# Hybrid attention and delta-rule layer on one core: where the modulation sums are kept, who splits the weights, and the order of every queue

## The chip, the cores and the metric

One of the eight cores of a Trainium2 chip runs the kernel. The metric is device time in microseconds (us) of one execution. Before the change it is 202.49 us, the median of three runs (202.23, 202.49, 203.05).

## The reference, cut to what matters

One layer over x of 256 rows and 1024 columns, batch 1, all in fp32:

```python
mod = silu(c) @ ada_w + ada_b                  # 1024 x 3072
shift, scale, gate = split(mod, 3)
h = rmsnorm(x, pre_norm_w) * (1 + scale) + shift
proj = h @ w_in                                # 1024 x 4104
# attention branch (8 heads of 64): rope on q and k, causal softmax, times silu(mg)
# delta branch (4 heads of 128, chunks of 64): short convolution over 4 rows, silu, l2 norm of
#   q and k, decays from db and da, solve of a 64 x 64 triangular system per chunk and head,
#   scan over the 4 chunks, rmsnorm, times silu(dz)
y = concat([o_moba, o_dn]) @ w_out             # 1024 x 1024
return x + gate * rmsnorm(y, post_norm_w)
```

## The kernel before, in words

Five engines run lists of calls that are written out by hand, one list each: SP issues the loads, PE (TensorE) multiplies, DVE (VectorE), ACT (ScalarE) and POOL (GpSimd) do the rest. An engine works strictly in the order of its list. A call waits for semaphores at its head, and all that stands behind it on its engine waits too.

**Split products.** fp32 products are made of three products of fp32r parts: each matrix is split in a high part (a copy, rounded to fp32r) and a low part (matrix minus high part), and `three` issues high*high, low*high and high*low. The weights come in 44 units. Unit n is copied to `whi` by ACT (`hi(n)`, L537) and its low part is made as `raw - whi` (`lo(n)`) by POOL (L459), or by DVE (L895) for the units that `DVE_LO` names: 41 to 43. Four split buffers are in turn, so `hi(n)` waits until PE has used unit n-4. Units 0 to 15 are the delta branch's q, k and v weights (384 KB, 768 columns, two units for each 128 rows of `w_in`), 16 to 35 are the rest of `w_in` (512 KB, 1024 columns), 36 to 43 are `w_out`.

**Modulation.** `silu(c) @ ada_w` for shift and scale is made in five pieces, which `PIECES` lists: pieces 0 and 1 give one 128-row block k of h each, pieces 2, 3 and 4 two. A piece has eight chunks (128 rows of `ada_w` each, 256 or 512 columns), loaded two at a time by `load_ada(p, g0, g1)`. DVE sums chunk times c_k over the chunks of `mod_sums` (L914, L916, L918); the running sum is in a PSUM bank (6 or 7), the last addition writes `acc` in SBUF. `mod(p)` on PE (L1341) then sums over partitions with a column of ones. Of piece 0 only chunks 0 and 1 go this way; chunks 2 to 7 are multiplied by PE itself with c as a one-column operand (`mod_direct`, L1333). `DVE_K` has the number of chunks that DVE sums. `modulate(p)` (DVE, L928 and L930) makes the scale and shift columns, `modulated(p)` (ACT, L580) applies them to the turned x, `h_hi(p)` (ACT, L585) and `h_lo(p)` (DVE, L885) split the result. `ada0` and `ada1` hold two pieces, so the loads of pieces 3 and 4 wait for the sums of pieces 1 and 2.

**Start.** x is scaled, turned by PE (`x_turn(b)`, L1325) into four banks and copied to `xT` by ACT (`xT_copy`) and DVE (`xT_move`). `qkv_products(n)` multiplies unit n (18 products of 256 columns) into six banks that hold all of q, k and v. Four of these banks held the turned x, so the first products wait for these copies. Unit n needs `h_lo` of its block and `lo(n)`. `busy(b, n)` issues products of ones that no one reads.

**Middle.** After `last_qkv_products`, `half(j)` multiplies unit 16+j (24 products of 256 columns); two halves make one of ten groups (attention q, k, v and the gates). Between the halves stand the small products of the delta branch: decays (`rows`, `cum`), the triangular inverse in levels 0 to 5 (`z_products`, `t_turn`, `x_products` on PE, `mask_z` and `merge` on DVE, `ti_copy` on ACT) for two row tiles, then the scan over four chunks; and the attention (`scores`, `probs`, `maxima`, `normalise`, `p_turn`, `pv`). `rope(r)` on DVE shuffles a group, POOL multiplies it by the sine (`rope_sin(r)`, L473), and DVE adds (L1061).

**End.** `y_products(k, t)` multiply `w_out` (6 products of 512 columns), `last_y_products` finish the second row tile, and `y_norm` and `finish` write the output.

## Time and profile before

| | before |
|---|---|
| median of three runs | 202.49 us |
| the profiled execution's own time | 202.14 us |
| its span, first to last instruction | 200.2 us |
| PE / DVE / ACT / POOL busy in the span | 188.3 / 135.5 / 103.7 / 95.1 us |
| DMA, mean over the span | 192 GB/s |
| mean granted TensorE clock | 0.982 of 2.4 GHz |

The profiled execution takes 1.94 us more than its span. Busy shares are averages over stages with different limits; a busy PE counts the modelled end of each product, and the products overlap: their starts in the trace stand 0.12 us apart where each shows 0.28 us. The granted clock has two levels, 1.0 (2.4 GHz) and 0.5 (1.2 GHz).

### The profile page before, as it was taken

The page shows a single profiled execution, that of the slowest core. Times are in us where ns is not written, and L with a number is a line of the kernel's source. Part 1 is how long each engine was busy: PE and PEld are TensorE (multiplying, and loading weights), DVE is VectorE, ACT ScalarE, POOL GpSimd, SP SyncE. Part 2 cuts the span into 40 slices and gives each one's busy share as a digit, 9 for nine tenths or more (in the row PEclk, how much of TensorE's full clock was granted, in tenths as well). Part 3 has the DMA queues.
Part 4 walks back from the last instruction along what each step waited for, and adds up shares of the span by engine and source line. Part 5 has one row for each costly group of instructions (what it writes and reads, how often), then busy time and mean ns, then how long its engine had stood idle before and what let it go on. Part 6 is the DMA issues. An engine that isn't in the chain of part 4 may idle for free.

```text
span 200.2 us, 4697 instructions
## 1 busy us (share of the span) xinstructions
PE 188.3 (94%) x1896; PEld 173.3 (87%) x1896; DVE 135.5 (68%) x315; ACT 103.7 (52%) x195; POOL 95.1 (47%) x51
## 2 busy tenths in 40 slices
PE   7998779999999989999999999999999999999970
PEld 6897769999999979989989998999899888788850
DVE  0657989472089976989868577938899256555364
ACT  3746344636379689754843432264651384463330
POOL 2037609795979348909372069540180072580000
PEclk9979999999999999999999999999999999999996
DMA  6999999997069800294300007105498735200022
GB/s 213 383 399 411 402 407 407 401 400 286 5 224 415 334 5 0 70 399 160 114 3 0 3 3 259 58 5 213 131 398 309 201 122 209 106 0 3 0 106 105
DMA packets 11527, 38.39 MB, mean 192 GB/s; under 512 B 1393, under 2 KB 1521, under 8 KB 10994
## 3 DMA queue, kind: packets, MB, share of 16 engines
q1 hardware_dynamic: 11362, 37.57, 49.5%
q10 hardware_dynamic: 144, 0.52, 0.7%
q8 instruction: 15, 0.25, 0.5%
q14 instruction: 6, 0.05, 0.1%
HBM read 37.04 MB, written 1.05 MB: 190 GB/s over the span
## 4 chain that ended last, share of the span: by engine, by line
PE 80%; DVE 15%; ACT 2%; issue 1%; POOL 1%; DVEq 0%; POOLq 0%
PE bank L1305 16%; PE bank L1307 15%; PE bank L1306 15%; DVE cv L941 6%; PE bank L1316 4%; DVE bank L916 3%; PE bank L1524 3%; PE bank L1513 3%; PE bank L1501 2%; PE bank L1325 2%; PE bank L1619 2%; PE bank L1595 2%; PE bank L1626 2%; PE bank L1561 1%; PE bank L1341 1%
## 5 line engine op out<-in xcount | busy, mean ns | idle before, releaser
L459 POOL TENSOR_TENSOR wlo<-raw,whi 128x1024 fp32r<-128x1024 f32 (+1 forms) x30 | 69.1, 2320 | 61.1 <-ACT whi L537 61.1
L1305 PE MATMUL bank<-hhi,whi 128*128 128x256 f32 x224 | 65.0, 290 | 2.5 <-DVE hlo L885 1.4
L1306 PE MATMUL bank<-hhi,wlo 128*128 128x256 f32 x224 | 63.3, 283 | 0.0
L1307 PE MATMUL bank<-hlo,whi 128*128 128x256 f32 x224 | 63.3, 283 | 0.0
L1305 PEld LDWEIGHTS bank<-hhi,whi 128*128 128x128 f32 x224 | 43.0, 192 | 4.1 <-DVE hlo L885 1.8
L1306 PEld LDWEIGHTS bank<-hhi,wlo 128*128 128x128 f32 x224 | 43.0, 192 | 0.0
L1307 PEld LDWEIGHTS bank<-hlo,whi 128*128 128x128 f32 x224 | 42.9, 191 | 0.0
L537 ACT ACTIVATE whi<-raw 128x1024 fp32r<-128x1024 f32 (+1 forms) x33 | 33.1, 1026 | 14.3 <-PE bank L1307 12.8
L941 DVE SCALAR_TENSOR_TENSOR cv<-bank,convh,cv 128x255 f32<-128x255 f32 (+2 forms) x36 | 17.0, 480 | 8.6 <-ACT cv L599 7.6
L916 DVE SCALAR_TENSOR_TENSOR bank<-ada,sml,bank 128x512 f32<-128x512 f32 (+1 forms) x24 | 16.5, 687 | 0.7
L1115 DVE SCALAR_TENSOR_TENSOR accg<-ada,sml,accg 128x512 f32<-128x512 f32 x16 | 13.6, 852 | 0.5
L1305 PE MATMUL bank<-whi,ohi 128*128 128x512 f32 x32 | 13.0, 406 | 0.0
L1306 PE MATMUL bank<-whi,olo 128*128 128x512 f32 x32 | 12.5, 390 | 0.0
L1307 PE MATMUL bank<-wlo,ohi 128*128 128x512 f32 x32 | 12.5, 390 | 0.0
L473 POOL TENSOR_TENSOR rot<-rot,cst 128x512 f32<-128x512 f32 x4 | 4.4, 1092 | 14.9 <-DVE rot L1057 11.7
L667 ACT ACTIVATE pr<-bank,stat 128x128 f32<-128x128 f32 (+1 forms) x16 | 6.5, 418 | 7.4 <-DVE stat L1082 7.4
L1316 PE MATMUL bank<-ones 128*128 128x256 f32 x26 | 8.5, 484 | 1.1 <-DVE ones L854 1.1
L580 ACT ACTIVATE bank<-xs,mod_b,mod_a 128x256 f32<-128x256 f32 x7 | 3.7, 561 | 10.7 <-DVE mod_a L930 10.7
L1305 PE MATMUL bank<-whi,hhi 128*128 128x256 f32 x32 | 9.1, 285 | 0.0
L1306 PE MATMUL bank<-whi,hlo 128*128 128x256 f32 x32 | 9.1, 283 | 0.0
L1307 PE MATMUL bank<-wlo,hhi 128*128 128x256 f32 x32 | 9.0, 283 | 0.0
L459 POOL TENSOR_TENSOR wlo<-cv,whi 128x768 fp32r<-128x768 f32 x4 | 7.3, 1846 | 2.2 <-ACT whi L537 2.0
(200 smaller groups left out, 359.2 us busy)
## 6 DMA issues: line engine op xcount, KB each, us to landing
raw<-in_w_rest SPq DMA_DIRECT2D x20, 512.0 KB, 5.6
ada<-in_ada SPq DMA_DIRECT2D x12, 512.0 KB, 9.0
ada<-in_gate_w SPq DMA_DIRECT2D x4, 1024.0 KB, 6.2
raw<-in_w_out SPq DMA_DIRECT2D x8, 512.0 KB, 4.5
ada<-in_ada SPq DMA_DIRECT2D x8, 256.0 KB, 6.1
raw<-in_w_qkv SPq DMA_DIRECT2D x5, 384.0 KB, 7.4
qkvs<-in_w_qkv SPq DMA_DIRECT2D x4, 384.0 KB, 9.4
cv<-in_w_qkv SPq DMA_DIRECT2D x4, 384.0 KB, 12.6
```

Of the source, the lines that this page charges most:

```text
L459: pool.tensor_tensor(split_u(wlo, n), raw_u(n), split_u(whi, n).bitcast(F32), ALU.subtract).then_inc(lo_done, 1)
L537: act.activation(split_u(whi, n), raw_u(n), ACT.Copy).then_inc(hi_done, 1)
L667: act.activation(pr[:, e, o:o + w], bank[ATT[e]][:, o:o + w], ACT.Exp, scale=AD ** -0.5, bias=stat[:, 16 + i:17 + i], accum_out=stat[:, 32 ...
L916: link(dve.scalar_tensor_tensor(a, w, c_k, a, ALU.mult, ALU.add))
L941: ins = dve.scalar_tensor_tensor(cv[:, i, j:], b[:, 0:S - j], w, cv[:, i, j:], ALU.mult, ALU.add)
L1115: dve.scalar_tensor_tensor(a, adag[:, k, :], sml[:, 24 + k:25 + k], a, ALU.mult, ALU.add).then_inc(gate_acc, 1)
L1305: pe.matmul(out, a[0][ia], b[0][ib], start=start, stop=False, skip_group_check=skip)
L1306: pe.matmul(out, a[1][ia], b[0][ib], start=False, stop=False, skip_group_check=skip)
L1307: return pe.matmul(out, a[0][ia], b[1][ib], start=False, stop=stop, skip_group_check=skip)
L1316: pe.matmul(bank[b][:, 0:256], ones[:, :], ones[:, 0:1].to_broadcast([P, 256]), start=True, stop=True)
L1513: ins = pe.matmul(blocks(3 + 2 * t, 0, CHUNK)[r, h, :], tt[r, t * DH + h, :], ident_of(c), start=True, stop=True)
L1524: ins = pe.matmul(blocks(2 + 2 * t, 256, HALF)[r, h, :], ti[r, i, :], zt[r, i, :], start=True, stop=True)
```

## The change

Five kinds of edit, made together:

1. `mod_sums` keeps the running sum in `acc` (SBUF) from the first chunk on. It no longer needs banks 6 and 7, so it no longer waits for `h_lo` of an earlier piece, only until `mod` has read `acc` of two pieces before.
2. Of pieces 1 and 2, chunks 6 and 7 are multiplied by PE (`mod_direct(p, k)`), as six chunks of piece 0 are; the bank that they write must be free (`mod_bank_free`). The loads of pieces 3 and 4 wait for these products too.
3. x block 0's turn moves ahead of chunks 6 and 7 of piece 0; the last two `busy` calls go.
4. The low parts of units 1 to 11, 13, 21, 26 and 37 move from POOL to DVE, that of unit 42 from DVE to POOL.
5. The lists of SP, ACT, DVE, PE and POOL get new orders. Units 1, 2 and 3 are loaded behind all of piece 2. On ACT `softplus` stands ahead of most tanh calls; on DVE `rope(0)` ahead of the silus; on PE the halves stand elsewhere among the small products, and the first two `y_products` are a little earlier.

The diff, cut to its core ("..." marks what is left out, all of it moved calls in the lists):

```diff
-        DVE_K = (2, 8, 8, 8, 8)
+        DVE_K = (2, 6, 6, 8, 8)
+
+        def directs(p):
+            return sum(NK - n for n in DVE_K[:p + 1])
...
-        DVE_LO = (41, 42, 43)
+        DVE_LO = (1, 2, 3, 4, 5, 6, 7, 8, 9, 10, 11, 13, 21, 26, 37, 41, 43)
...
                 if p == 3 and g0 == 0:
                     sp.wait_ge(acc_done, 2)
-                    sp.wait_ge(direct_done, NK - DVE_K[0])
+                    sp.wait_ge(direct_done, directs(1))
                 if p == 4 and g0 == 0:
                     sp.wait_ge(acc_done, 3)
+                    sp.wait_ge(direct_done, directs(2))
...
             load_ada(0, 2, 4)
+            load_ada(1, 0, 2)
             load_unit(0)
-            load_ada(1, 0, 2)
-            load_unit(2)
-            load_unit(1)
             load_ada(1, 2, 4)
-            load_unit(3)
             load_ada(2, 0, 2)
             load_ada(2, 2, 4)
+            load_unit(1)
+            load_unit(2)
+            load_unit(3)
+            load_ada(3, 0, 2)
             load_unit(4)
-            load_ada(3, 0, 2)
-            load_unit(6)
+            load_gates()
             load_unit(5)
             load_ada(3, 2, 4)
+            load_unit(8)
+            load_unit(6)
             load_unit(7)
-            load_unit(8)
             load_ada(4, 0, 2)
             load_unit(10)
+            load_gate_bias()
+            load_unit(12)
             load_unit(9)
             load_ada(4, 2, 4)
+            load_unit(16)
             load_unit(11)
-            load_unit(12)
...
             lo(31)
+            rope_sin(3)
             lo(32)
             lo(33)
             lo(34)
             lo(35)
             lo(36)
-            lo(37)
             lo(38)
             lo(39)
             lo(40)
+            lo(42)
...
             modulated(0)
-            xT_copy(0)
             h_hi(0)
+            xT_copy(1)
             xT_copy(2)
             hi(1)
+            xT_copy(0)
             hi(2)
             hi(3)
             modulated(1)
             h_hi(1)
-            xT_copy(1)
...
             conv_tanh(0)
+            softplus()
             conv_tanh(1)
             conv_tanh(2)
             conv_tanh(3)
-            softplus()
+            taps(4)
+            taps(5)
             hi(21)
...
-                n = 256 * PIECES[p][1]
-                a = bank[6 + p % 2][:, 0:n]
-                if p == 1 and k0 == 0:
-                    dve.wait_ge(mod_read, 1)
+                a = acc[:, p % 2, 0:256 * PIECES[p][1]]
                 if p >= 2 and k0 == 0:
-                    dve.wait_ge(hlo_done, p - 1)
-                for k in range(k0, k1):
+                    dve.wait_ge(mod_ready, p - 1)
+                for k in range(k0, min(k1, DVE_K[p])):
                     w, c_k = ada_piece(p)[:, k, :], sml[:, 24 + k:25 + k]
                     if k % 2 == 0:
                         dve.wait_ge(*ada_ready(p, k))
                     if k == 0:
-                        link(dve.tensor_scalar(a, w, c_k, None, ALU.mult))
-                    elif k < DVE_K[p] - 1:
-                        link(dve.scalar_tensor_tensor(a, w, c_k, a, ALU.mult, ALU.add))
+                        ins = dve.tensor_scalar(a, w, c_k, None, ALU.mult)
                     else:
-                        dve.scalar_tensor_tensor(acc[:, p % 2, 0:n], w, c_k, a, ALU.mult, ALU.add).then_inc(acc_done, 1)
+                        ins = dve.scalar_tensor_tensor(a, w, c_k, a, ALU.mult, ALU.add)
+                    if k < DVE_K[p] - 1:
+                        link(ins)
+                    else:
+                        ins.then_inc(acc_done, 1)
...
                 dve.wait_ge(mod_ready, p + 1)
+                dve.wait_ge(direct_done, directs(p))
                 if p == 0:
-                    dve.wait_ge(direct_done, NK - DVE_K[0])
                     dve.wait_ge(scale_done, 1)
...
             mod_sums(0, 0, 2)
             x_rstd()
             x_scale()
+            mod_sums(1, 0, 4)
             columns_in()
             modulate(0)
-            mod_sums(1, 0, 4)
             h_lo(0)
             xT_move(3)
-            mod_sums(1, 4, 8)
+            mod_sums(2, 0, 4)
+            mod_sums(1, 4, 6)
+            mod_sums(2, 4, 6)
+            lo(1)
             modulate(1)
-            mod_sums(2, 0, 4)
+            lo(2)
+            lo(3)
             h_lo(1)
-            mod_sums(2, 4, 8)
             mod_sums(3, 0, 2)
             modulate(2)
             mod_sums(3, 2, 4)
+            lo(4)
             h_lo(2)
+            lo(5)
             mod_sums(3, 4, 8)
+            lo(6)
             mod_sums(4, 0, 2)
             modulate(3)
+            lo(7)
+            lo(8)
             h_lo(3)
             mod_sums(4, 2, 4)
+            lo(9)
             mod_sums(4, 4, 8)
+            lo(10)
             ba_lo()
+            lo(11)
             modulate(4)
             h_lo(4)
+            lo(13)
...
-            conv_silu(0)
-            conv_silu(1)
             gates_in()
             rope(0)
+            conv_silu(0)
+            gates_out()
+            conv_silu(1)
             conv_silu(2)
-            gates_out()
             conv_silu(3)
             cum_copy()
             rope(1)
+            lo(21)
             conv(4)
...
             conv(5)
+            columns()
             conv_silu(4)
...
-            k_tokens(0)
             row_sum(0)
             maxima(0)
+            k_tokens(0)
+            k_tokens(1)
...
             decayed(0)
             decayed(1)
+            v_tokens(0)
+            v_tokens(1)
+            mask_z(0, 0)
+            mask_z(0, 1)
             gated_heads(0)
-            mask_z(0, 0)
+            mask_z(1, 0)
+            q_decayed(0)
+            mask_z(1, 1)
+            lo(26)
+            q_decayed(1)
...
             state_update(1)
             gate(2)
             gate(3)
+            o_sums(0)
+            lo(37)
             state_update(2)
-            gated_heads(3)
...
             lo(41)
-            lo(42)
             lo(43)
...
-            def mod_direct(k):
-
-                pe.wait_ge(sc_done, 1)
-                pe.wait_ge(*ada_ready(0, k))
-                for i in range(2):
-                    ins = pe.matmul(bank[7][:, i:i + 1], ada_piece(0)[:, k, i * P:(i + 1) * P], sml[:, 24 + k:25 + k],
-                                    start=(k == DVE_K[0] and i == 0), stop=False, skip_group_check=True)
+            def mod_bank_free(p):
+
+                if p == 1:
+                    pe.wait_ge(mod_read, 1)
+                if p >= 2:
+                    pe.wait_ge(hlo_done, p - 1)
+
+            def mod_direct(p, k):
+
+                if p == 0:
+                    pe.wait_ge(sc_done, 1)
+                if k == DVE_K[p]:
+                    mod_bank_free(p)
+                pe.wait_ge(*ada_ready(p, k))
+                for i in range(2 * PIECES[p][1]):
+                    ins = pe.matmul(bank[mod_bank(p)][:, i:i + 1], ada_piece(p)[:, k, i * P:(i + 1) * P], sml[:, 24 + k:25 + k],
+                                    start=(k == DVE_K[p] and i == 0), stop=False, skip_group_check=True)
                 ins.then_inc(direct_done, 1)
 
             def mod(p):
 
                 pe.wait_ge(acc_done, p + 1)
+                if DVE_K[p] == NK:
+                    mod_bank_free(p)
                 for i in range(2 * PIECES[p][1]):
                     ins = pe.matmul(bank[mod_bank(p)][:, i:i + 1], acc[:, p % 2, i * P:(i + 1) * P], ones[:, 0:1],
-                                    start=(p > 0), stop=True, skip_group_check=(p == 0))
+                                    start=(DVE_K[p] == NK), stop=True, skip_group_check=(DVE_K[p] < NK))
                 ins.then_inc(mod_ready, 1)
...
             busy(1, 3)
             busy(3, 8)
-            mod_direct(2)
-            mod_direct(3)
-            busy(2, 1)
-            mod_direct(4)
+            mod_direct(0, 2)
+            mod_direct(0, 3)
+            mod_direct(0, 4)
+            mod_direct(0, 5)
             mod(0)
-            mod_direct(5)
-            busy(0, 1)
-            mod_direct(6)
-            mod_direct(7)
             x_turn(0)
+            mod_direct(0, 6)
+            mod_direct(0, 7)
             x_turn(1)
             x_turn(2)
             x_turn(3)
             qkv_products(0)
+            mod_direct(1, 6)
+            mod_direct(1, 7)
+            mod_direct(2, 6)
             mod(1)
+            mod_direct(2, 7)
+            mod(2)
             qkv_products(1)
             qkv_products(2)
-            mod(2)
             qkv_products(3)
             qkv_products(4)
...
+            cum()
             k_turn(0)
-            cum()
-            k_turn(1)
             q_turn(0)
             q_turn(1)
+            k_turn(1)
             half(4)
```

## Rows read from the trace of the kernel before

**Rows 1.** The page, busy time of PE, and the engines' shares of the last-ending chain.
```profile
PE 188.3 (94%) x1896; PEld 173.3 (87%) x1896; DVE 135.5 (68%) x315; ACT 103.7 (52%) x195; POOL 95.1 (47%) x51
...
PE 80%; DVE 15%; ACT 2%; issue 1%; POOL 1%; DVEq 0%; POOLq 0%
```
**Rows 2.** Timeline of PE, 15 to 31 us: start, duration, work, [idle before, releaser].
```profile
18.35 0.61 PE L1341 MATMUL bank<-ones,acc 128*128 128x1 f32 x4 [0.58 <-DVE acc L918]
...
20.84 0.39 PE L1305 MATMUL bank<-hhi,whi 128*128 128x256 f32 x1 [1.07 <-ACT xs L567]
...
22.83 0.39 PE L1305 MATMUL bank<-hhi,whi 128*128 128x256 f32 x1 [0.29 <-DVE hlo L885]
...
25.86 1.05 PE L1341 MATMUL bank<-ones,acc 128*128 128x1 f32 x8 [0.61 <-DVE acc L918]
...
30.27 0.39 PE L1305 MATMUL bank<-hhi,whi 128*128 128x256 f32 x1 [1.11 <-DVE hlo L885]
```
**Rows 3.** The chain that ended last: the sums of piece 4 over partitions.
```profile
44.38 0.79 PE bank L1341 x8
```
**Rows 4.** Timeline of DVE, 13 to 43 us: sums of one-block and two-block pieces, h_lo.
```profile
16.25 1.53 DVE L916 SCALAR_TENSOR_TENSOR bank<-ada,sml,bank 128x256 f32<-128x256 f32 x3
...
29.53 0.69 DVE L885 TENSOR_TENSOR hlo<-bank,hhi 128x512 fp32r<-128x512 f32 x1 [0.37 <-ACT hhi L585]
30.13 2.33 DVE L916 SCALAR_TENSOR_TENSOR bank<-ada,sml,bank 128x512 f32<-128x512 f32 x3
...
42.47 0.75 DVE L918 SCALAR_TENSOR_TENSOR acc<-ada,sml,bank 128x512 f32<-128x512 f32 x1
```
**Rows 5.** Line L1115, the gate's sums in SBUF: count, shortest/median/longest ns.
```profile
L1115 DVE SCALAR_TENSOR_TENSOR accg<-ada,sml,accg x16: 740/752/2376, 128.7 to 154.7; 128x512 f32<-128x512 f32 x16
```
**Rows 6.** Timelines of ACT and PE, 10 to 22 us: unit 0, turned x, units 1 to 4.
```profile
10.21 0.84 ACT L537 ACTIVATE whi<-raw 128x768 fp32r<-128x768 f32 x1 [0.32 <-DMA raw<-in_w_qkv]
...
21.92 0.84 ACT L537 ACTIVATE whi<-raw 128x768 fp32r<-128x768 f32 x1 [1.13 <-DMA raw<-in_w_qkv]
...
12.01 3.60 PE L1325 MATMUL bank<-cst,xn 128*128 128x128 f32 x16
15.26 0.48 PE L1305 MATMUL bank<-hhi,whi 128*128 128x256 f32 x1
```
**Rows 7.** Stretches of 1 us: five engines busy, granted clock, DMA share, GB/s.
```profile
12.00:13.00 1.00, 1.00 (x7) 1.00 (x7) 0.72 (x3) 0.00 (x0) 0.94 (x1) 0.55 1.04 407
...
15.00:16.00 1.00, 1.00 (x8) 1.00 (x7) 0.44 (x2) 1.00 (x2) 0.00 (x0) 0.75 1.05 421
```
**Rows 8.** Timelines of POOL and DVE: the low parts of units, 768 and 1024 columns.
```profile
48.15 5.47 POOL L459 TENSOR_TENSOR wlo<-cv,whi 128x768 fp32r<-128x768 f32 x3 [2.02 <-ACT whi L537]
...
185.72 1.23 DVE L895 TENSOR_TENSOR wlo<-raw,whi 128x1024 fp32r<-128x1024 f32 x1 [2.85 <-ACT whi L537]
```
**Rows 9.** Timelines of POOL and DVE: calls of both engines that overlap in time.
```profile
42.31 1.85 POOL L459 TENSOR_TENSOR wlo<-rot,whi 128x768 fp32r<-128x768 f32 x1
...
117.95 7.49 POOL L459 TENSOR_TENSOR wlo<-raw,whi 128x1024 fp32r<-128x1024 f32 x3
...
43.52 0.73 DVE L890 TENSOR_TENSOR wbs<-wba,wbs 128x64 fp32r<-128x64 f32 x1 [0.29 <-ACT wbs L589]
...
118.09 2.80 DVE L1061 TENSOR_TENSOR kT<-rot 128x512 f32<-128x512 f32 x1 [0.76 <-POOL rot L473]
```
**Rows 10.** Timelines of DVE and PE, 55 to 76 us: the convolutions and what follows.
```profile
55.63 11.99 DVE L941 SCALAR_TENSOR_TENSOR cv<-bank,convh,cv 128x255 f32<-128x255 f32 x24 [7.56 <-ACT cv L599]
...
73.42 0.36 PE L1427 MATMUL bank<-zz,cst 128*128 128x8 f32 x2 [0.89 <-DVE zz L970]
...
75.64 0.36 PE L1305 MATMUL bank<-hhi,whi 128*128 128x256 f32 x1
```
**Rows 11.** The chain that ended last: half(8) from its start to the next call.
```profile
89.91 0.32 PE bank L1305
92.97 0.44 PE bank L1466 x4
```

More of the change, by code:

```diff
@@ L786, in _ @@
             decays(0)
+            factors()
+            v_copy(0)
+            hi(27)
             probs(0)
             decays(1)
[L789 removed]
             pT_copy(0)
[L791 removed]
+            ti_copy(1, 0)
+            ti_copy(1, 1)
+            probs(1)
             hi(28)
             hi(29)
[L794 to L796 removed]
             hi(30)
+            hi(31)
             ti_copy(2, 0)
             ti_copy(2, 1)
[L800 to L801 removed]
             ti_copy(3, 0)
             ti_copy(3, 1)
+            pT_copy(1)
             ti_copy(4, 0)
             hi(32)
[L806 removed]
             hi(33)
[L808 to L810 removed]
             ti_copy(4, 1)
             ti_copy(5, 0)
+            probs(2)
+            ti_copy(5, 1)
             v_copy(1)
+            heads_hi(0)
             pT_copy(2)
[L815 removed]
+            gate_tanh(1)
             wT_copy(0)
@@ L818, in _ @@
             hi(34)
+            wT_copy(1)
             hi(35)
+            heads_hi(1)
             probs(3)
-            wT_copy(1)
-            heads_hi(2)
+            hi(36)
+            hi(37)
+            vnew_copy(1)
             gate_tanh(2)
-            vnew_copy(1)
             pT_copy(3)
             gate_tanh(3)
-            hi(36)
-            hi(37)
+            hi(38)
             vnew_copy(2)
@@ L831, in _ @@
             vnew_copy(3)
-            hi(38)
+            hi(39)
+            heads_hi(2)
+            heads_hi(3)
             o_norm(1)
-            heads_hi(3)
-            hi(39)
             dn_hi(0)
+            hi(40)
             dn_hi(1)
-            hi(40)
             hi(41)
@@ L1249, in _ @@
             merge(2, 1)
-            rope(3)
             mask_z(3, 0)
             mask_z(3, 1)
-            gated_heads(1)
             merge(3, 0)
             merge(3, 1)
-            q_decayed(1)
+            rope(3)
+            gated_heads(1)
+            gate_sums(0, 0, 4)
             mask_z(4, 0)
             maxima(2)
-            gate_sums(0, 0, 4)
+            gate_sums(0, 4, 8)
+            merge(4, 0)
             mask_z(4, 1)
-            merge(4, 0)
-            normalise(2)
             mask_z(5, 0)
             merge(4, 1)
+            mask_z(5, 1)
+            normalise(2)
+            merge(5, 0)
+            gate_sums(1, 0, 4)
+            heads_lo(0)
             gate(1)
-            heads_lo(0)
-            merge(5, 0)
-            mask_z(5, 1)
-            gate_sums(0, 4, 8)
             gated_heads(2)
-            heads_lo(1)
             merge(5, 1)
@@ L1732, in _ @@
             half(8)
+            half(9)
             rows(1)
-            half(9)
+            kk_products(0)
+            kk_products(1)
             v_turn(0)
@@ L1737, in _ @@
             p_turn(0)
-            kk_products(0)
-            kk_products(1)
-            pv(0)
             z_products(0, 0)
             z_products(0, 1)
+            pv(0)
+            z_products(1, 0)
+            z_products(1, 1)
+            t_turn(1, 0)
+            t_turn(1, 1)
             scores(1)
+            x_products(1, 0)
+            x_products(1, 1)
             half(10)
             half(11)
-            z_products(1, 0)
-            t_turn(1, 0)
-            t_turn(1, 1)
-            z_products(1, 1)
-            x_products(1, 0)
-            x_products(1, 1)
+            p_turn(1)
+            z_products(2, 0)
             t_turn(2, 0)
-            z_products(2, 0)
             t_turn(2, 1)
@@ L1757, in _ @@
             x_products(2, 1)
+            z_products(3, 0)
             t_turn(3, 0)
             t_turn(3, 1)
-            z_products(3, 0)
             z_products(3, 1)
-            p_turn(1)
-            half(12)
-            pv(1)
             x_products(3, 0)
             x_products(3, 1)
+            t_turn(4, 0)
+            t_turn(4, 1)
             z_products(4, 0)
-            z_products(4, 1)
-            t_turn(4, 0)
+            pv(1)
+            half(12)
             scores(2)
@@ L1772, in _ @@
             half(13)
-            half(15)
             x_products(4, 0)
-            t_turn(4, 1)
+            z_products(4, 1)
             t_turn(5, 0)
@@ L1779, in _ @@
             x_products(5, 0)
+            z_products(5, 1)
             t_turn(5, 1)
-            z_products(5, 1)
+            half(15)
             p_turn(2)
```

129 lines of the change are left out of this document (44 added, 85 removed).

## The prediction

> **What bounds the kernel now.** I read the page first: PE is busy for 188.3 of 200.2 us, and the chain that ended last runs through PE for 80% of it [rows 1]. So only time in which PE stands still, or runs at the low clock, can be won; work moved between the other engines counts only by what PE waits for. The timeline of PE shows where it stands still: between its first unit product at 15.26 and 30.27 it waits five times, for sums (0.58 and 0.61), for a bank that still holds turned x (1.07) and for low parts of h (0.29 and 1.11), 3.66 us in all [rows 2]. From 30.27 on the timeline shows one more wait of note, 0.89 us at 73.42 for the decays [rows 10]. In between PE is never short of work: it comes to the sums of piece 4 at 44.38, though DVE had made them at 42.47 + 0.75 = 43.22 [rows 3, 4]. Last the stretches: the granted clock falls from 2.4 to 1.2 GHz at 12.1 us and is back at 15.5, in the middle of the stretch from 15 us [rows 7].
>
> The start is thus a race: PE's work until the sums of piece 4 ends at 44.38, and DVE is 1.16 us ahead of it. The change can give back PE's 3.66 us of waits only as far as DVE gets ready earlier, and it also gives DVE more to do.
>
> **The first product.** x is turned until 12.01 + 3.6 = 15.6 now, and unit 0 starts at 15.26 [rows 6]. With block 0's turn ahead of two chunks and two fillers gone, the 16 turns start near 10.3 and end near 13.8, the last eight at the low clock. Unit 0 is loaded behind two chunks of piece 1 (2 x 256 KB; at 400 GB/s, as the stretches show [rows 7], 1.3 us), so its high part starts at 10.21 + 1.3 = 11.5 and ends at 12.4; POOL's low part takes 1.82 us, a third of 5.47 [rows 8], and ends at 14.25. DVE's h_lo(0) ends near 14.05: it sums four chunks of piece 1 first (4 x 0.51 by 1.53 for three [rows 4], from 9.9 to 11.9), then modulates. Unit 0 starts at 14.3, 1 us earlier.
>
> **Loads.** Unit 4 lands at 21.9 [rows 6], behind units 1 to 3 and piece 2. The same bytes now come with the units last: unit 3 at 21.9 - 1.0 = 20.9, unit 2 at 19.9, unit 1 at 19.0. PE has no unit between 17.1 and 19. That costs nothing by itself, since DVE makes the sums of pieces 1 and 2 in this time, and PE's added work lies here as well: chunks 6 and 7 of pieces 1 and 2 are 8 + 16 one-column records, and four take 0.5 to 0.61 [rows 2], so 3.0 to 3.7 us, between 17.1 and 21.3.
>
> **DVE's queue from 14.05 to the last sum of piece 4.** I add it up, since I find no wait of more than a few tenths in it (each chunk lands before its turn):
> - xT_move: 0.6.
> - Sums: six of piece 2 and eight each of pieces 3 and 4, 22 x 0.78 = 17.2 (2.33 for three [rows 4]), and two of piece 1, 1.0. That these now read and write SBUF is priced at nothing: the gate's sums of the same width do so with a median of 752 ns [rows 5], against 750. The four sums taken off DVE (2 x 0.51 + 2 x 0.78 = 2.6) are already left out.
> - Low parts of units 1 to 9: no row shows 768 columns on DVE; 1024 take 1.23 [rows 8], 512 take 0.69 [rows 4], so 0.95, with starts 0.9 apart: 8.1. Bounds: the starts of 512 and of 1024 columns, 0.6 and 1.2, so 5.4 to 10.8.
> - modulate(1) to (3) 0.95, h_lo(1) to (3) 1.55.
>
> Sum 29.4, end at 43.45; now it is 43.22. DVE saves 2.6 and an earlier start, and spends 8.1 on low parts. PE meanwhile: h_lo(2) falls at 28.5 in this queue, unit 4 starts there and not at 30.27, units 4 to 9 take 6 x 2.16 (18 x 0.12) and the sums of piece 3 0.9, so PE is done at 42.4 and waits 1 us for DVE. mod(4) starts at 43.5 and not at 44.38: **lead 0.9 us**. Of the 3.66 us of waits three quarters come back as waits for DVE. With the bounds of the low part DVE ends between 40.8 and 46.2; below 42.4 PE sets the time, so the lead is between 2.0 and -1.8.
>
> **From there to 76 us.** Low parts on DVE take half as long as on POOL (0.95 for 1.82), PE needs one per 2.16 us: no wait. The convolutions, 11.99 us on DVE [rows 10], start with the last q, k, v products, so the lead goes through them. Behind them the order is new: gates_in 0.85, rope(0) 2.8, a silu 0.6, gates_out 0.35, three silus 1.8, the copy of the sums 0.2, then PE's three turns 1.4, as the same calls take now in other order. That is 8.0 us, no less than now (67.62 to 75.64), from the convolutions' end at 67.6 - 0.9 = 66.7, so the next half starts at 74.8 and not at 75.64 [rows 10]: lead 0.8. The wait of 0.89 becomes a wait for the silus.
>
> **Behind 76 us.** The amount of PE work is the same, only its order differs. A half that follows small products takes 92.97 - 89.91 = 3.06 [rows 11] against 24 x 0.12 = 2.88, 0.18 more; the change puts halves 8 and 9 side by side, which gives back one such entry, and lays three levels of the inverse bare that had a half between them. I take zero. The low part of unit 42 moves to POOL (2.4 for 1.23) some 2 us ahead of need; nothing waits. The tail is untouched.
>
> **Sum.** 202.14 - 0.8 = 201.3 for a profiled execution. This one lies 0.35 under the median, so the median goes from 202.49 to **201.7 us**; the likeliest case's own range is 200.6 to 202.4.
>
> **A rule weighed.** While POOL makes a low part, a DVE call with two SBUF inputs doesn't run: the 64-column L890 took 0.73 us, started at 43.52 and ended as POOL's call did (44.16), and L1061, 0.69 elsewhere, took 2.80 beside POOL's three [rows 9]. The Trainium skill says the same (SBUF — State Buffer, "SBUF: two separate sides"): the shared port pair is an exclusive lock, also for a DVE operation with two SBUF inputs against a GpSimd one that reads SBUF, and whichever starts first holds it for the whole instruction. By this rule the sums in SBUF are free only while POOL is idle, and it is from 14.3 to 44 us. The trace agrees. The places where POOL is not idle are the second rival.
>
> **Rivals.**
> - *The new orders give PE back its small gaps.* For: 0.18 us at each entry to a half, twelve halves behind 76 us, together 2.2. Against: it needs every handover to be covered better, and the levels laid bare are not. 201.7 - 2.2 = 199.5.
> - *DVE waits for POOL at the low part of unit 21 (slower).* DVE reaches lo(21) behind rope(1), at 76.2 by my walk; ACT ends the high part of unit 22 at 76.4, and POOL then holds SBUF for 2.4 us. If POOL comes first, lo(21) ends at 76.4 + 2.4 + 1.2 = 80.0 and not at 77.4; PE needs it at 74.8 + 2.9 = 77.7, and waits 2.3 us. It decides from a shift of 0.2 us. 201.7 + 2.3 = 204.0. The same can happen at ba_lo beside lo(12), near 44 us, for 0.5 to 1.3 us more. For: L1061 in [rows 9]. Against: order at this place is a near tie.
> - *The clock falls in the start.* Before 12.1 us PE did mostly one-column products, and the clock fell [rows 7]. PE now does such products, and waits, from 17.1 to 21.3. At 1.2 GHz from 18.9 to 25.7 units 1 and 2 take 4.3 each: PE reaches unit 4 near 30, lead 0.3, so 202.2. A single such stretch of 3.4 us is hidden by DVE's queue.
>
> **How the numbers follow.** A measurement here can tell about 0.5%, 1.0 us. Forecast 0.35, small gaps won 0.26, DVE behind POOL 0.27, clock 0.12. Faster by over 1.0: nearly all of the gaps case, and 0.4 of the forecast's, 0.14: 0.40. Slower by over 1.0: nearly all of the POOL case, and the low part's upper bound: 0.26. Within: 0.34. The range is 199.2 to 204.5.
>
> **What would show it.** After: unit 0 near 14.3; unit 4 near 28.5; PE waiting about 1 us for L1341 near 42.5 to 43.5 with DVE without idle time ahead of it; sums in `acc` at 0.75 us; low parts of 768 columns at 0.95. L895 for unit 21 at 1.2 us (3.6 would be the POOL case), and half(5) without idle time ahead. The granted clock between 18 and 26 us at 1.0, or 0.5 for the clock case. The forecast is wrong if DVE's queue isn't what mod(4) waits for, or if PE takes a different time from 76 us to its last product than the 118 us of now.

## The result: 214.5 us, 5.9% slower, and the profile after

The changed kernel takes 214.47 us (median of four runs, 213.50 to 215.30). The kernel before took 202.36 us beside it (202.14 to 203.05). The ratio is 1.059, with a 95% interval of 1.054 to 1.065. Here and below a median and a range are over all executions of a kernel, a ratio leaves out those more than 1.5% above its fastest. The forecast was 201.7 us, with a range of 199.2 to 204.5: wrong in sign and in size. The profiled execution took 213.66 us.

The page of the kernel after, its span, the busy times and the shares of the chain that ended last; to be read beside [rows 1]:

```profile
span 211.9 us, 4737 instructions
...
PE 194.4 (92%) x1916; PEld 178.9 (84%) x1916; DVE 149.9 (71%) x325; ACT 103.7 (49%) x195; POOL 69.6 (33%) x37
...
PEclk9999589999999999999999859999999999999996
...
PE 61%; DVE 18%; issue 7%; DMA 5%; ACT 4%; SPq 3%; POOL 1%; DVEq 0%; ACTq 0%
```

The span grew by 11.7 us, PE's busy time by 6.1 us. So about half of the loss is PE standing still, and the other half is PE being busy for longer. Part of that are the one-column products that it has taken over, the larger part is in the clock's row: the slices of 5.3 us each show 5 tenths at the fifth, and 8 and 5 at the 23rd and 24th. The chain has PE in it for 61% (80% before) and DVE for 18% (15%).

The waits of PE in the kernel after name the first half (engine and line, what it waited for, us in total, times, longest):

```profile
PE bank L1642 <- DVE pr L1080: 7.5, 1, 7.5
PE bank L1320 <- DVE ones L845: 1.1, 1, 1.1
PE bank L1455 <- DVE gcs L965: 0.9, 1, 0.9
```

One wait of 7.5 us: the turns of p (`p_turn(1)`, L1642) for `normalise(1)` on DVE (L1080), which scales the four p tiles of a head pair. Of line L1080 the trace of the kernel after gives the shortest, median and longest call:

```profile
L1080 DVE TENSOR_SCALAR pr<-pr,stat x16: 272/346/2448, 97.6 to 161.5; 128x128 f32<-128x128 f32 x8, 128x256 f32<-128x256 f32 x8
```

Sixteen calls, half of them under 0.35 us, and the longest, of 256 columns, 2.45 us where such a call takes 0.35 otherwise. The timelines of the kernel after at this place say why, DVE first, then POOL, ACT and PE (start, duration, work, [idle before, releaser]):

```profile
112.02 0.69 DVE L1051 TENSOR_TENSOR qT<-rot 128x512 f32<-128x512 f32 x1 [0.76 <-POOL rot L478]
112.63 0.17 DVE L1076 RECIPROCAL stat<-stat 128x4 f32<-128x4 f32 x1
112.84 9.35 DVE L1080 TENSOR_SCALAR pr<-pr,stat 128x128 f32<-128x128 f32 x4
122.11 0.47 DVE L1036 TENSOR_TENSOR tt<-tt,bank 128x128 f32<-128x128 f32 x2
...
110.83 1.09 POOL L478 TENSOR_TENSOR rot<-rot,cst 128x512 f32<-128x512 f32 x1 [12.65 <-issue]
112.68 9.35 POOL L464 TENSOR_TENSOR wlo<-raw,whi 128x1024 fp32r<-128x1024 f32 x4 [0.77 <-ACT whi L528]
...
111.54 2.96 ACT L528 ACTIVATE whi<-raw 128x1024 fp32r<-128x1024 f32 x3
114.85 1.06 ACT L528 ACTIVATE whi<-raw 128x1024 fp32r<-128x1024 f32 x1 [0.35 <-PE bank L1311]
...
114.48 0.28 PE L1311 MATMUL bank<-hlo,whi 128*128 128x256 f32 x1
...
122.24 1.11 PE L1642 MATMUL bank<-cst,pr 128*128 128x128 f32 x4 [7.48 <-DVE pr L1080]
```

Four scalings on DVE and four low parts on POOL take the same 9.35 us, from the same moment: each scaling waits until a low part is done (9.35 / 4 = 2.34 us), then the next low part starts, then the next scaling waits. The low parts take what they take alone (2.4 us), so DVE alone pays. Moves in two lists of the change open the door. On POOL `rope_sin(3)` stood ahead of `lo(29)` and waited for DVE's shuffle, and now stands behind `lo(31)`; `lo(28)` stood ahead of `rope_sin(2)` and now stands behind it, so that there are four low parts in a row. And `hi(28)`, `hi(29)` stood ahead of `probs(1)` on ACT and now stand behind it, so ACT delivers 28, 29 and 30 in one go from 111.54, just as DVE comes to `normalise(1)`. POOL and DVE of the kernel before, at the same place:

```profile
116.90 1.09 POOL L473 TENSOR_TENSOR rot<-rot,cst 128x512 f32<-128x512 f32 x1 [8.19 <-DVE rot L1057]
...
109.63 1.01 DVE L1090 TENSOR_SCALAR pr<-pr,stat 128x128 f32<-128x128 f32 x4
```

POOL stood idle for 8.19 us in front of `rope_sin(3)`, and in that idle time the four scalings ran in 1.01 us. What looks like a useless wait kept POOL out of DVE's way. Nor has PE other work in the kernel after: its list has `p_turn(1)` ahead of two levels of the inverse, whose `merge` (L1036) is queued behind the scalings on DVE as well.

The second half, in stretches of the kernel after (length, then per engine busy us (calls) in the order PE, PEld, DVE, ACT, POOL, then granted clock, DMA share, GB/s):

```profile
20.00:21.00 1.00, 1.00 (x10) 1.00 (x11) 1.00 (x3) 0.90 (x3) 0.00 (x0) 0.92 0.92 298
21.00:27.00 6.00, 6.00 (x29) 6.00 (x30) 5.86 (x14) 3.30 (x6) 0.00 (x0) 0.50 1.01 374
27.00:28.00 1.00, 1.00 (x7) 1.00 (x7) 0.55 (x2) 0.97 (x3) 0.00 (x0) 0.66 1.00 377
...
119.00:120.00 1.00, 0.00 (x0) 0.00 (x0) 1.00 (x2) 0.00 (x0) 1.00 (x2) 0.92 0.00 0
120.00:126.00 6.00, 3.76 (x48) 3.43 (x50) 2.87 (x4) 0.27 (x1) 2.03 (x1) 0.50 0.48 170
126.00:127.00 1.00, 1.00 (x31) 1.00 (x28) 0.00 (x0) 0.50 (x2) 0.00 (x0) 0.67 0.86 242
```

While PE stands still the clock goes to 1.2 GHz, at 119.8 (by the 0.92 of the stretch from 119), and stays there until 126.7. PE works from 122.2 to 126.7 at half rate: 4.5 us of time for 2.2 us of work, so 2.2 us more. The clock is low in the start as well, from 20.8 to 27.7, as the clock rival said; the low stretch that the kernel before has from 12.1 to 15.5 is not there in this execution.

The rest of the loss lies in the start. Timelines of DVE, POOL and PE of the kernel after, around the sums of piece 4, with PE's half(8) and its last product:

```profile
42.26 2.33 DVE L904 SCALAR_TENSOR_TENSOR acc<-ada,sml,acc 128x512 f32<-128x512 f32 x3
...
45.37 1.86 DVE L881 TENSOR_TENSOR wbs<-wba,wbs 128x64 fp32r<-128x64 f32 x1
47.15 0.95 DVE L886 TENSOR_TENSOR wlo<-rot,whi 128x768 fp32r<-128x768 f32 x1
...
57.38 1.00 DVE L931 SCALAR_TENSOR_TENSOR cv<-bank,convh,cv 128x255 f32<-128x255 f32 x2 [5.51 <-ACT cv L590]
...
44.92 2.23 POOL L464 TENSOR_TENSOR wlo<-cv,whi 128x768 fp32r<-128x768 f32 x1 [30.57 <-ACT whi L528]
...
44.74 0.95 PE L1357 MATMUL bank<-ones,acc 128*128 128x1 f32 x8
...
91.86 0.39 PE L1309 MATMUL bank<-hhi,whi 128*128 128x256 f32 x1
...
205.35 0.39 PE L1311 MATMUL bank<-wlo,ohi 128*128 128x512 f32 x1
```

mod(4) starts at 44.74 and not at 44.38 [rows 3]. `ba_lo` (L881, 64 columns) takes 1.86 us beside POOL's low part of unit 12 and pushes back the low part that PE needs next; the convolutions start at 57.38 and not at 55.63 [rows 10], half(8) at 91.86, where the timeline of before has 89.84: 2.0 us late. The stall adds 7.6 (114.48 to 122.24, less the 0.12 of a product), the clock behind it 2.2: 11.8 us in all. PE's last product moved from 193.72 to 205.35, by 11.6.

### The profile page after: what moved, and what is told of

Read it like the earlier page. It is cut to its first block, busy times and chain, and to the rows that moved or that the text cites. A ratio compares the mean times of both kernels' runs of the same rounds, so it can differ in the third digit from the quotient of the medians.

```text
span 211.9 us, 4737 instructions
## 1 busy us (share of the span) xinstructions
PE 194.4 (92%) x1916; PEld 178.9 (84%) x1916; DVE 149.9 (71%) x325; ACT 103.7 (49%) x195; POOL 69.6 (33%) x37
## 4 chain that ended last, share of the span: by engine, by line
PE 61%; DVE 18%; issue 7%; DMA 5%; ACT 4%; SPq 3%; POOL 1%; DVEq 0%; ACTq 0%
PE bank L1309 14%; PE bank L1311 13%; PE bank L1310 13%; DVE cv L931 5%; DMA ada<-in_ada 5%; DVE pr L1080 4%; SPq L342 3%; PE bank L1529 2%; PE bank L1540 2%; DVE wlo L886 2%; PE bank L1517 2%; DVE acc L904 2%; PE bank L1611 1%; PE bank L1642 1%; PE bank L1577 1%
## 5 line engine op out<-in xcount | busy, mean ns | idle before, releaser
L464 POOL TENSOR_TENSOR wlo<-raw,whi 128x1024 fp32r<-128x1024 f32 (+1 forms) x24 | 57.6, 2416 | 61.6 <-ACT whi L528 61.6
L1310 PE MATMUL bank<-hhi,wlo 128*128 128x256 f32 x224 | 64.6, 288 | 0.0
L1311 PEld LDWEIGHTS bank<-hlo,whi 128*128 128x128 f32 x224 | 44.2, 197 | 0.0
L904 DVE SCALAR_TENSOR_TENSOR acc<-ada,sml,acc 128x512 f32<-128x512 f32 (+1 forms) x25 | 17.1, 686 | 0.7
L464 POOL TENSOR_TENSOR wlo<-cv,whi 128x768 fp32r<-128x768 f32 x3 | 5.9, 1985 | 35.1 <-ACT whi L528 35.1
L886 DVE TENSOR_TENSOR wlo<-raw,whi 128x1024 fp32r<-128x1024 f32 (+1 forms) x9 | 9.8, 1100 | 5.5 <-ACT whi L528 5.5
L1080 DVE TENSOR_SCALAR pr<-pr,stat 128x128 f32<-128x128 f32 (+1 forms) x16 | 12.9, 864 | 0.1
L634 ACT ACTIVATE ti<-bank 128x256 f32<-128x256 f32 x10 | 3.8, 382 | 17.0 <-PE bank L1529 16.9
L1642 PE MATMUL bank<-cst,pr 128*128 128x128 f32 x24 | 4.1, 314 | 7.5 <-DVE pr L1080 7.5
L1642 PEld LDWEIGHTS bank<-cst,pr 128*128 128x128 f32 x24 | 3.1, 161 | 7.8 <-DVE pr L1080 7.7
```

The source lines that it names most:

```text
L464: pool.tensor_tensor(split_u(wlo, n), raw_u(n), split_u(whi, n).bitcast(F32), ALU.subtract).then_inc(lo_done, 1)
L886: dve.tensor_tensor(split_u(wlo, n), raw_u(n), split_u(whi, n).bitcast(F32), ALU.subtract).then_inc(dve_lo_done, 1)
L904: ins = dve.scalar_tensor_tensor(a, w, c_k, a, ALU.mult, ALU.add)
L1080: ins = dve.tensor_scalar(pr[:, e, o:o + w], pr[:, e, o:o + w], stat[:, i:i + 1], None, ALU.mult)
L1310: pe.matmul(out, a[1][ia], b[0][ib], start=False, stop=False, skip_group_check=skip)
L1311: return pe.matmul(out, a[0][ia], b[1][ib], start=False, stop=stop, skip_group_check=skip)
```

## Experiments

The theories have letters in the expectations. A: the 10 us behind 110 us come from POOL's pile of low parts meeting normalise(1), and the lower clock that follows from it. B: POOL has no part in it. C: the near tie of `ba_lo` with the low part of unit 12 (in experiment 5 C is another theory, told there, and in experiment 6 the tie is under A). D: TensorE's clock in the start. The times before in the same sets were 202.1 to 202.3 us.

**1. POOL yields to normalise(1).** The change, plus one wait on POOL:

```diff
             rope_sin(2)
+            pool.wait_ge(pn_done, 2)    # until normalise(1) is done
             lo(28)
```

> The changed kernel, with one wait more: POOL starts the low part of unit 28 only when normalise(1) on DVE is done. Theory A (port): in the changed kernel the four scalings of normalise(1) each wait for one of POOL's four low parts of units 28 to 31, 9.35 us where they take 1.0 otherwise, and PE's 7.6 us of idle time before p_turn(1) and the 1.2 GHz stretch behind it come from that. Then normalise(1) takes 1.0 us, PE's idle time goes, and the time is 214.5 - 7.6 - 2.2 = 204.7 us (203.5 to 206), 1 to 2% slower than before. Theory B (order): p_turn(1) and level 2 of the inverse stand too early in PE's list for DVE, whatever POOL does: the stall stays over 4 us and the time over 210.

Measured: 203.75 us (201.64 to 208.37, ten runs), ratio 1.003 (1.000 to 1.007). One wait gives back 10.7 of the 12.1 us. The timelines of this kernel, DVE and POOL:

```profile
111.03 1.01 DVE L1081 TENSOR_SCALAR pr<-pr,stat 128x128 f32<-128x128 f32 x4
```
```profile
112.12 9.32 POOL L464 TENSOR_TENSOR wlo<-raw,whi 128x1024 fp32r<-128x1024 f32 x4 [2.01 <-DVE pr L1081]
```

The four scalings take 1.01 us, the low parts their 9.32 as before, only behind them. A holds. From `p_turn(1)` to PE's last product this kernel takes 81.06 us (112.77 to 193.83) and the changed one 83.11 (122.24 to 205.35), 2.05 more, which is the price of the clock behind the stall, 2.2 by the sum above. In this execution `ba_lo` came first and took 0.22 us, the convolutions started at 55.61 and PE's last product at 193.83, against 193.72 before. Its clock was low in the start for 6.8 us in all, as in the changed kernel, but in two stretches, 11.2 to 14.7 and 21.5 to 24.9.

**2 and 3. Each half of the change alone.** The start of the change (up to the last q, k, v product) with the rest of before, and the reverse. The part that differs, beside the lists:

```diff
-        DVE_LO = (41, 42, 43)
+        DVE_LO = (1, ..., 11, 13, 41, 42, 43)   # front alone
+        DVE_LO = (21, 26, 37, 41, 43)           # back alone
```

> The change in the start alone: sums in SBUF, chunks 6 and 7 of pieces 1 and 2 on PE, the new orders up to the last q, k, v products, and the low parts of units 1 to 11 and 13 on DVE; from there on the lists of before. In the changed kernel the convolutions start 1.75 us later than before (57.38 against 55.63), so both theories expect 202.4 + 1.8 = 204.2 us (203.3 to 205). Were the start better than before once the rest is as it was, it would be under 202.

> The start of before, and from the last q, k, v products on the lists of the change (units 21, 26, 37 on DVE, 42 on POOL). Theory A: the meeting of normalise(1) with POOL's low parts is still there, so 202.4 + 7.6 + 2.2 = 212.2 us (210 to 213.5). If the meeting hangs on a shift of a microsecond at the start, it is under 207.

Measured: front alone 203.64 us (200.80 to 205.59, ten runs, four of them between 200.8 and 201.5 and none from there to 203.6), ratio 0.999 (0.995 to 1.003). Back alone 212.82 (212.03 to 214.84), ratio 1.053 (1.047 to 1.060). The waits of PE in the kernel with the back alone have the stall of the full change:

```profile
PE bank L1626 <- DVE pr L1088: 7.5, 1, 7.5
```

So the loss sits in the back half. The start has two values: four executions are about 1.1 us faster than the kernel before, six are 1.3 or more slower, and the median is that of the slower ones, just inside the 203.3 to 205 that I expected.

**4. The pile without the change.** The kernel before, with `rope_sin(3)` out of the way and `lo(28)` kept back, so that three low parts meet DVE in the same place:

```diff
-            lo(28)
             start_inverse()
             rope_sin(2)
-            rope_sin(3)
+            pool.wait_ge(rope_done, 3)
+            lo(28)
             lo(29)
             lo(30)
+            rope_sin(3)
             lo(31)
```

> The kernel before, in which POOL waits until rope(2) is done and then makes the low parts of units 28, 29 and 30 in a row (rope_sin(3) behind them): nothing else is changed, and PE needs unit 28 only some 15 us later. Theory A: three of the four scalings of normalise(1) each wait for 2.4 us, normalise(1) takes 7 to 8 us for 1.0, merge(1, 0) behind it on DVE is late, PE waits 5 to 7 us: 207 to 211 us. Theory B: POOL is a bystander, 202.4 us, within 0.5%.

Measured: 210.63 us (209.03 to 211.80), ratio 1.039 (1.034 to 1.043). The timelines of DVE and POOL, then the waits of PE:

```profile
109.34 7.31 DVE L1091 TENSOR_SCALAR pr<-pr,stat 128x128 f32<-128x128 f32 x4
```
```profile
109.30 7.01 POOL L459 TENSOR_TENSOR wlo<-raw,whi 128x1024 fp32r<-128x1024 f32 x3 [0.87 <-DVE qT L1062]
```
```profile
PE bank L1525 <- DVE zt L1034: 4.6, 1, 4.6
```

The meeting alone, with no other part of the change, costs 8 us. PE waits for a level of the inverse here, since in the order of before it is that which is queued behind the scalings. The profiled execution (211.80, 9.7 us over before's 202.14) adds up: PE waits 4.6 us, and the clock is low from 116.8 to 127.0 beneath working PE, 5.1 us at half rate.

**5. Half the dose.** The change, with two low parts ahead of the wait and two behind:

```diff
             lo(28)
             lo(29)
+            pool.wait_ge(pn_done, 2)
             lo(30)
```

> The changed kernel; POOL makes the low parts of units 28 and 29 at once and waits for normalise(1) only ahead of unit 30, so two of the four low parts can meet it. Theory A (port): normalise(1) takes 9.35 - 2 x 2.1 = 5.2 us, PE idles about 3.4 us before p_turn(1); 214.5 - 4.2 - up to 2.2 for the clock = 208 to 210.5 us. Theory C (the meeting decides as a whole, as a fixed delay of the first call): 204 or 214, no value in between.

Measured: 209.64 us (208.70 to 210.35), ratio 1.036 (1.033 to 1.039). DVE of this kernel:

```profile
112.61 5.17 DVE L1081 TENSOR_SCALAR pr<-pr,stat 128x128 f32<-128x128 f32 x4
```

5.17 us for the four: two meetings of 2.35 and two calls of some 0.25. The price is per meeting, as the alternation of single calls says, and theory C of this experiment is refuted. The kernel is 7.6 us over the one before, and not the half of 12.1: PE waits 3.3 us for L1081, and the clock falls all the same, from 119.3 to 126.1 in this execution, all of it beneath working PE, which is 3.4 us at half rate, where the full stall hid a part of it.

**6. The tie in the start as well.** Experiment 1, plus a wait for the low part of unit 12:

```diff
+            pool.wait_ge(dve_lo_done, 11)
             lo(12)
```

> The changed kernel with two waits on POOL: unit 28's low part behind normalise(1), and unit 12's behind DVE's low part of unit 11, so that ba_lo can't meet it (1.86 us in the changed kernel's trace, 0.22 in the trace of the run with the first wait alone). Theory A: the start's scatter is this near tie; executions of 203 to 208 us go, and the median falls from 203.7 to about 202 (201.3 to 202.8). Theory D: the scatter is the TensorE clock alone, then the median stays at 203 to 204 and single executions still reach 205.

Measured: 203.71 us (201.38 to 205.37, twelve runs), ratio 1.005 (1.002 to 1.007). `ba_lo` takes 0.22 us in its profile, but the scatter stays and the median is that of experiment 1: what theory D expected, and not A. In the profiled execution, of 204.46 us, the stretches show the clock low twice:

```profile
21.00:27.00 6.00, 6.00 (x29) 6.00 (x30) 5.86 (x13) 3.37 (x7) 0.00 (x0) 0.50 1.01 385
...
75.00:76.00 1.00, 1.00 (x6) 1.00 (x7) 1.00 (x2) 1.00 (x3) 0.36 (x1) 0.63 0.00 0
76.00:78.00 2.00, 2.00 (x12) 2.00 (x11) 1.24 (x3) 2.00 (x3) 1.28 (x2) 0.50 0.00 0
```

**7. Front alone, without the tie.** Experiment 2 plus the wait for unit 12:

> The change's start with the rest of before, as in the run with the front alone, and GpSimd's low part of unit 12 now waits until VectorE's low part of unit 11 is done, so that the cast of ba's low part cannot meet it. Theory C (the near tie at 45 us costs what lies between 55.6 and 57.2 us at the first convolution): every execution lands near the lower of the two values of the front alone, 201.2 to 202.3 us. Theory D (the scatter is TensorE's granted clock in the start alone): executions near 203.6 remain, and the median stays at 202.5 to 203.8 us.

Measured: 201.83 us (200.80 to 205.63, twelve runs), ratio 0.9964 (0.9943 to 0.9985): faster than the kernel before by 0.4%, the only version here whose interval lies below 1. Both theories hold in part. The two profiled executions, of experiments 2 and 7, have the clock low for 6.8 us each, 0.4 us apart (from 20.1 and from 20.5); DVE's timelines differ in `ba_lo` and in what follows, experiment 2 first:

```profile
45.22 1.86 DVE L883 TENSOR_TENSOR wbs<-wba,wbs 128x64 fp32r<-128x64 f32 x1
57.24 3.07 DVE L933 SCALAR_TENSOR_TENSOR cv<-bank,convh,cv 128x255 f32<-128x255 f32 x6 [5.52 <-ACT cv L592]
```
```profile
45.22 0.22 DVE L884 TENSOR_TENSOR wbs<-wba,wbs 128x64 fp32r<-128x64 f32 x1
55.95 6.44 DVE L934 SCALAR_TENSOR_TENSOR cv<-bank,convh,cv 128x255 f32<-128x255 f32 x13 [5.88 <-ACT cv L593]
```

The convolutions start 1.29 us earlier, and the executions took 203.65 and 202.35 us, 1.30 apart: that is the price of the tie (C). The executions of experiment 7 still fall in two groups, six from 200.8 to 201.4 and five from 202.2 to 202.6, and one of 205.6. Only one was profiled, at 202.35 with the clock low from 20.5 to 27.3 and a mean granted clock of 0.976. Four of the lower six have a mean of 0.974 to 0.976, so their clock was low for as long. If D explains the two groups, it does so by where the low stretches fall, as in experiment 1, where they came in two; that is argued, not shown.

**8. Four fillers against the clock.** Experiment 6, with products of ones among the one-column products:

```diff
             mod_direct(1, 7)
+            keep_warm(1)                # busy(3, 1)
             mod_direct(2, 6)
+            keep_warm(1)
             mod(1)
+            keep_warm(1)
             mod_direct(2, 7)
+            keep_warm(1)
             mod(2)
```

> As the run with two waits, and four calls of products of ones (each two records of 0.22 us on a free bank) among PE's one-column products between 16.7 and 21.7 us. The clock theory: the granted clock stays at 2.4 GHz from 18 to 28 us (it was at 1.2 GHz from 20.85 to 27.68 in the changed kernel), unit 1 starts 0.9 to 1.3 us later but units 1 and 2 take 2.2 us each; DVE's queue then sets mod(4) near 44 us, so the gain over the run with two waits is 0 to 1 us, and the scatter is smaller: median 201 to 202, all executions within 1.5 us. If the low clock there costs nothing, the median is 0.5 us above the run with two waits.

Measured: 204.37 us (201.61 to 211.12, twelve runs), ratio 1.004 (1.001 to 1.007). A miss: the clock is low all the same in the profiled execution, from 21.6 to 28.4 us, and the convolutions start at 57.34 where experiment 6 has 55.98. Three executions near 211 us have a mean granted clock of 0.945 to 0.947, the profiled one 0.966: their clock was low for longer. Where, and why, stays open.

**9. No one-column products of pieces 1 and 2.** Experiment 7, with all sums on DVE as before:

```diff
-        DVE_K = (2, 6, 6, 8, 8)
+        DVE_K = (2, 8, 8, 8, 8)
```

> The front alone with the wait of unit 12, but without TensorE's one-column products for chunks of pieces 1 and 2: VectorE sums all chunks of these pieces, as before. Theory D (the one-column products bring the fall of the clock at 20 to 27 us): no half clock between 20 and 28 us, but VectorE's queue is longer by some 2.6 us, so mod(4) is late by some 2 us: 203.5 to 204.5 us. Rival (the clock falls from the waits for pieces, not from the products): half clock there as well, and 205 to 206 us.

Measured: 204.56 us (204.45 to 204.63, four runs), ratio 1.010 (1.009 to 1.012). The time is 2.7 us over experiment 7, close to the 2.6 us that DVE has to sum more; its last sum ends at 46.50 and not at 44.43. The stretches of this kernel:

```profile
17.00:19.00 2.00, 0.00 (x0) 0.00 (x0) 1.88 (x4) 0.01 (x1) 0.00 (x0) 1.00 1.04 405
19.00:21.00 2.00, 0.61 (x4) 0.52 (x4) 1.93 (x4) 1.90 (x4) 0.00 (x0) 1.00 0.81 232
21.00:22.00 1.00, 0.00 (x0) 0.00 (x0) 0.96 (x2) 0.78 (x1) 0.00 (x0) 0.74 0.55 127
22.00:28.00 6.00, 5.07 (x24) 5.08 (x24) 5.89 (x14) 2.14 (x4) 0.00 (x0) 0.50 1.04 412
```

The clock falls here too, at 21.5, after PE has worked for only 0.6 of the 4.5 us before. My expectation that it would stay up was wrong: it falls at this place with one-column products and with next to no work. As PE stands still here where it had those products, the run can't tell whether the products alone would bring the fall. The four executions lie within 0.2 us, which fits DVE's queue being the bound, whatever PE's clock does.

**10. The sums in SBUF alone.** The kernel before with only the first edit of the change, POOL keeping all its low parts (the waits for banks 6 and 7 move from DVE to `mod` on PE, as in the change):

```diff
-                a = bank[6 + p % 2][:, 0:n]
...
+                a = acc[:, p % 2, 0:n]
...
-                    dve.wait_ge(hlo_done, p - 1)
+                    dve.wait_ge(mod_ready, p - 1)
```

> The kernel before with one part of the change alone: the modulation sums are kept in SBUF, and POOL still makes the low parts of units 0 to 15. Port theory: each DVE addition has two SBUF inputs and waits for POOL's low part when one runs; POOL makes eleven of 1.85 us between 11 and 46 us beside 29 additions, so DVE's sums end 6 to 12 us later, PE waits at the pieces, and the time is 206 to 212. If sums in SBUF cost what they do in PSUM (0.75 us each) whatever POOL does: 202 or a little less, since mod_sums waits less.

Measured: 219.21 us (218.44 to 219.84), ratio 1.084 (1.081 to 1.086), worse than I expected. DVE, POOL and the waits of PE in this kernel:

```profile
16.05 5.96 DVE L914 SCALAR_TENSOR_TENSOR acc<-ada,sml,acc 128x256 f32<-128x256 f32 x3
...
47.94 9.69 DVE L914 SCALAR_TENSOR_TENSOR acc<-ada,sml,acc 128x512 f32<-128x512 f32 x5
```
```profile
15.99 5.74 POOL L459 TENSOR_TENSOR wlo<-raw,whi 128x768 fp32r<-128x768 f32 x3 [3.25 <-ACT whi L537]
```
```profile
PE bank L1343 <- DVE acc L916: 11.6, 3, 4.7
```

Three sums take 5.96 us beside POOL's three low parts, where three took 1.53 with the running sum in a PSUM bank [rows 4]. The running sum in PSUM was what kept DVE clear of POOL in the start; the change can do without it only because it takes POOL out of the start.

**11. Back alone, without the meeting.** Experiment 3 plus the wait of experiment 1:

> The start of before with the change's lists and orders behind the convolutions, as in the run with the back alone, and GpSimd's low part of unit 28 waits for normalise(1) on VectorE. Theory A (all that the back half costs is the meeting of GpSimd's low parts with the four scalings of normalise(1)): 202.4 us, 201.5 to 203.3, so the new orders themselves are worth nothing either way. Rival (the moved turns of p cost by themselves, because nothing covers TensorE there): 204 us or more.

Measured: 203.20 us (202.13 to 204.98, twelve runs), ratio 1.005 (1.002 to 1.008). Six executions lie from 202.13 to 202.67, as before; the other six from 203.7 to 205.0. The profiled one is of the second kind (203.91):

```profile
75.00:76.00 1.00, 1.00 (x9) 1.00 (x8) 0.90 (x2) 1.00 (x2) 0.53 (x1) 0.75 0.00 0
76.00:78.00 2.00, 2.00 (x11) 2.00 (x10) 1.33 (x2) 2.00 (x3) 1.29 (x2) 0.50 0.00 0
78.00:79.00 1.00, 1.00 (x7) 1.00 (x6) 0.96 (x3) 1.00 (x4) 1.00 (x1) 0.54 0.00 0
```

From 75.5 to 78.9 us PE runs at 1.2 GHz (3.4 us, so 1.7 of work lost), behind a wait of 0.89 us and small products. The orders behind the convolutions are worth nothing without this, and cost 1.7 us with it. Which of the moved calls brings it was not tried, nor is it shown that any does: this execution has no low stretch in the start, where the kernel before has one of the same 3.4 us (12.1 to 15.5). There it seems to cost nothing: of the 23 executions of before beside this experiment, the six with a mean granted clock of 0.994 or 0.995 took 202.33 to 202.47 us, the fourteen with 0.981 to 0.985 took 201.85 to 202.30.

## Why the prediction was wrong, step by step

- **"Behind 76 us ... I take zero"** is the step that failed. It counted PE's work and its entries to halves, and did not walk the lists of ACT, POOL and DVE against each other. As far as PE's own order goes it was near: experiment 1 ends PE's work at 193.83 against 193.72, and half the executions of experiment 11 are those of before. What was missing is a meeting at 112.7 us that costs 7.6 us, and 2.2 more by the clock; experiments 1, 3, 4 and 5 show it from four sides. Of the 12.8 us between forecast and result it is 9.8; the start has most of the rest, with half(8) 2.0 us later where 0.8 earlier was forecast.
- **The rule weighed** was right and was applied too narrowly. I read it as a matter of calls with two SBUF inputs, and looked for them near POOL's moved low parts. L1080 has one large SBUF input, a scalar column and an SBUF output, and it waits too (2.34 us a call), as L881 does with two. The Trainium skill has the lock also for DVE operations in a two-port mode (SBUF — State Buffer, "SBUF: two separate sides"); the 9.35 us for four scalings agree with that, and that L1080 runs in such a mode is my reading of it, no row says so outright. Its rate fits: 0.28 us for 128 columns and 0.35 for 256 when it runs alone, 0.5 ns a column, where the sums with two inputs take 0.49 for 256 and 0.75 for 512, 1.0 ns a column. And the first chunk's scaling of 512 columns, the same operation, takes 0.48 us into SBUF (L902) and took 0.74 into a PSUM bank (L914 in the kernel before). In the kernel before POOL was idle while this line (L1090 there) ran, all its sixteen calls took 0.28 to 0.35 us, and [rows 9] could not show it. That `rope_sin(3)` moved behind three low parts could be read from the diff.
- **The rival "DVE waits for POOL at the low part of unit 21"** named the mechanism and a wrong place. DVE came first there, and its call took 1.22 us at 78.86. Its second place, `ba_lo` beside the low part of unit 12, did occur: priced at 0.5 to 1.3 us, 1.30 measured (experiment 7).
- **The clock rival** occurred for the 6.8 us that it named, 2 us later: low from 20.8 to 27.7 where I wrote 18.9 to 25.7. With the clock low, mod(4) is 0.36 us later than before, where I had 0.3 earlier. That it follows from the one-column products alone is not shown: without them the clock falls at this place too (experiment 9), but there PE stands still instead.
- **The walk through the start** was right in its sizes. Unit 0 started at 14.50 (14.3), low parts of 768 columns took 0.95, the sums in SBUF 0.75, and DVE's last sum ended at 44.6 where 43.45 was forecast, with a wait of 1.66 us for PE, behind its low stretch, in it. What it had wrong is who waits for whom: unit 4 started at 30.89 and not at 28.5, since units 1 and 2 took 4.0 and 3.0 us at the low clock for 2.16, and the wait of PE for mod(4), forecast as 1 us, did not occur; PE was busy without a gap from 30 to 45 us. Without the tie the start gives 0.4 us in the median, and 1.2 in the lower group of executions; the lead forecast was 0.8 to 0.9.
- **"The sums in SBUF are free only while POOL is idle"** was right, and experiment 10 gives the price if it isn't: 17 us.

## What to carry to other kernels

When a call moves on one engine, walk the other engines' lists past the new place and note which GpSimd and VectorE calls can now run at once. A short VectorE call that works in SBUF as those here do (two inputs, or the scaling of one) costs up to a whole GpSimd call at each meeting, and a pile of calls on both sides alternates one by one; sums with an input in PSUM did not wait (1.53 us for three beside a low part, against 5.96). Where the order cannot be seen to be safe, one wait that lets the short calls go first costs nothing if GpSimd has slack: here it was worth 10.7 us. An idle stretch of TensorE can cost more than its length, since the clock may be low behind it: 2.2 us behind 7.5 here, 3.4 behind 3.3 in experiment 5, 5.1 behind 4.6 in experiment 4.

## What the hardware showed that I had not expected

- VectorE's scaling of a 128x256 tile, SBUF to SBUF with one tensor input, waits for a running GpSimd tensor_tensor: 2.45 us at most for a call of 0.35 us (kernel after, L1080).
- The clock fell after 5 us of an idle PE at 119.8 (kernel after), but also at 75.5 behind an idle time of only 0.89 us among small products (experiment 11; the kernel after has the same wait, L1455 for `gcs`, and no fall), and at 20.8 with PE busy in one-column products (kernel after). Four pairs of filler products did not hold it up (experiment 8).
- The same kernel takes about 201.0 or 202.4 us from one execution to the next (experiment 7), where the kernel before has 201.85 to 202.87 in 23 executions.
